# One more token tile, one less row buffer, and vector sums and routing moved between stages of a gated encoder block with product-key experts

## What is computed

```
h = x + (sig(gA) * Pool(xn) W_po + sig(gB) * Hyena(xn) W_ho) W_o,  xn = rmsnorm(x)
PEER:  q = rmsnorm(h) W_q;  s = q . keys   (8 heads, 2 halves, 128 keys each)
       top 16 of each half, then top 16 of the 256 sums -> 128 experts a token
       gate = softmax over each head's 16
       y = sum_e  gelu(u[idx_e] . xb) * gate_e * v[idx_e]
out = rmsnorm(h + y)
```

## Time and profile before

| | |
|---|---|
| median of 3 runs | 3104.2 us (3100.14 to 3113.33) |
| the profiled execution | 3101.03 us |
| its span, first to last instruction | 3098.9 us |
| granted TensorE clock, mean | 0.935 |
| TensorE / VectorE / ScalarE / GpSimd busy | 2656.7 / 2259.4 / 1064.1 / 1085.0 us |
| bytes moved by DMA | 998.59 MB, 322 GB/s over the span |
| fetches of rows | 640, 671.13 MB |

### The profile page before, as it was taken

One profiled execution on the slowest core, in us unless ns is written; L12 is line 12 of the kernel. 1 busy time (PEld: TensorE's weight loads), 2 busy tenths in 40 slices (PEclk: granted clock), 3 DMA queues, 4 the chain that ended last, 5 costly groups with the idle time before them and its releaser, 6 DMA issues.

```text
span 3098.9 us, 29223 instructions
## 1 busy us (share of the span) xinstructions
PE 2656.7 (86%) x9109; PEld 1651.5 (53%) x9109; DVE 2259.4 (73%) x4295; ACT 1064.1 (34%) x2757; POOL 1085.0 (35%) x694
## 2 busy tenths in 40 slices
PE   6999989698899988899567899889889988899884
PEld 4556647443344444455245566556566555566662
DVE  5341124776799894487987899878789997778778
ACT  4211122231234885774383222223222222223221
POOL 2211212132344332223333344434444444344443
PEclk9999999899899999999788999999999999999997
DMA  4332255397899999888899999999999999999997
GB/s 153 112 102 72 89 180 173 140 400 287 332 359 371 356 333 362 351 326 350 301 388 364 378 404 402 380 393 391 386 382 404 409 404 377 388 408 396 400 397 291
DMA packets 246385, 998.59 MB, mean 322 GB/s; under 512 B 20856, under 2 KB 99448, under 8 KB 161753
## 3 DMA queue, kind: packets, MB, share of 16 engines
q0 software_dynamic: 92160, 671.13, 54.3%
q1 hardware_dynamic: 152344, 300.45, 26.9%
q10 hardware_dynamic: 1728, 25.17, 2.0%
HBM read 950.26 MB, written 46.40 MB: 322 GB/s over the span
## 4 chain that ended last, share of the span: by engine, by line
PE 26%; DVE 22%; DMA 18%; issue 9%; ACT 4%; SPq 1%; POOL 0%; DVEq 0%; ACTq 0%
DMA arena<-in_peer_ut 13%; DVE h_tile L1803 8%; PE job_ps L1561 6%; DVE row L1792 5%; PE job_ps L687 4%; PE job_ps L1548 3%; DMA row<-in_peer_uv,row_u 2%; PE wide_ps L128 2%; PE wide_ps L129 2%; PE wide_ps L130 2%; PE wide_ps L687 2%; PE job_ps L1524 2%; DMA tmp_gates<-arena 1%; DVE uw_lo L1812 1%; ACT uw_hi L1663 1%
## 5 line engine op out<-in xcount | busy, mean ns | idle before, releaser
L1493 POOL DMA_INDIRECT row<-in_peer_uv,row_u x640 | 966.8, 1511 | 1506.2 <-DVE h_tile L1803 1101.5
L1792 DVE CUSTOM_DVE_ANT_0 row<-row,x_tile 128x1024 f32<-128x1024 f32 x640 | 778.3, 1219 | 124.2 <-DMA row<-in_peer_uv,row_u 106.3
L1561 PE MATMUL job_ps<-arena 128*128 128x512 f32 x1536 | 682.9, 594 | 10.6 <-DVE arena L1823 10.6
L1803 DVE SCALAR_TENSOR_TENSOR h_tile<-row,act_e,h_tile 128x1024 f32<-128x1024 f32 x512 | 654.4, 1278 | 13.4 <-ACT act_e L1680 12.8
L1676 ACT ACTIVATE gelu_e<-dots 128x1 f32<-128x1 f32 x640 | 128.2, 200 | 1230.5 <-DVE dots L1792 1230.0
L128 PE MATMUL wide_ps<-x_hi,uw_lo 128*128 128x384 f32 x1024 | 391.2, 382 | 156.0 <-DVE uw_lo L1812 155.3
L1561 PEld LDWEIGHTS job_ps<-arena 128*128 128x128 f32 x1536 | 290.2, 190 | 319.9 <-issue 308.6
L130 PE MATMUL wide_ps<-x_hi,uw_hi 128*128 128x384 f32 x1024 | 357.1, 349 | 0.0
L129 PE MATMUL wide_ps<-x_lo,uw_hi 128*128 128x384 f32 x1024 | 356.6, 348 | 0.0
L128 PEld LDWEIGHTS wide_ps<-x_hi,uw_lo 128*128 128x128 f32 x1024 | 203.4, 199 | 222.4 <-DVE uw_lo L1812 208.1
L1548 PE MATMUL job_ps<-row,diag 128*128 128x512 f32 x512 | 260.6, 640 | 54.9 <-ACT diag L1687 54.9
(11 more groups left out here) (252 smaller groups left out, 3026.8 us busy)
## 6 DMA issues: line engine op xcount, KB each, us to landing
arena<-in_peer_ut SPq DMA_DIRECT2D x128, 512.0 KB
arena<-in_peer_v SPq DMA_DIRECT2D x128, 512.0 KB
hand<-tmp_gates SPq DMA_DIRECT2D x32, 768.0 KB
tmp_gates<-arena ACTq DMA_DIRECT2D x10, 2048.0 KB
arena<-in_w_in SPq DMA_DIRECT2D x32, 512.0 KB, 3.5
hand<-in_w_in SPq DMA_DIRECT2D x32, 512.0 KB
row<-in_peer_uv,row_u POOLq DMA_INDIRECT x640
arena<-in_x SPq DMA_DIRECT2D x16, 512.0 KB, 5.8
```

The lines of the kernel that those rows point to most:

```text
L1493: pool.indirect_dma_start(row[n % NR][:], None, dram["peer_uv"], bass.IndirectOffsetOnAxis(row_u[g % 2][:, e:e + 1], 0)).then_inc(row_in[n ...
L1561: last = pe.matmul(job_ps[q][:], actd[j % 2][:, d * P:(d + 1) * P], vw[j % NO][:, half * 512:(half + 1) * 512], start=j == 0, stop=j == P - 1)
L1792: dve.tensor_tensor_reduce(out=mine, in0=mine, in1=xb[:], scale=1.0, scalar=0.0, op0=ALU.mult, op1=ALU.add, accum_out=dots[:, n % NA:n % N ...
L1803: dve.scalar_tensor_tensor(out=side, in0=row[n % NR][:, D:2 * D], scalar=act_e[:, n % NA:n % NA + 1], in1=side, op0=ALU.mult, op1=ALU.add) ...
```

## The change

Seven edits, made together:

1. `NR` goes from 7 row buffers to 6.
2. The token tile `x_tile` gets two buffers with a semaphore each. `load_x(g)` is issued 40 steps before the tile is needed instead of 1, and waits for the dots of the group before the last one instead of the last dot.
3. `by_pe` changes by quarters of 64 fetches: 1 of 4, 2 of 4, 2 of 4, 3 of 4 rows go to TensorE, instead of every second. There are still 128 of them: 48 of the first tile and 80 of the second. `sum_row` finds its first and last row of a tile from the counts.
4. A unit of kinds z, a, x, ga, gb and q of the second sequence is issued on TensorE in two parts of four products, so that other work of the loop can stand between them.
5. Routing of dense tile 3 starts at step 134 instead of 106; its exponentials move from 143 to 171, its gates from 147 to 175.
6. The 16 chunks of tile 3 move with them, from steps 159 to 204 to steps 178 to 223. The chunks of the other tiles stay, and so does everything after step 256.
7. The final sum of TensorE's part (`gathered`) asks for `g < 2` instead of the last row's kind.

```diff
--- before.py
+++ after.py
@@ -607,6 +607,8 @@
                 self.weight_ready(pe, wi)
                 self.free(pe, kind, n)
                 for k in range(KD):
+                    if self.ready and k == KD // 2:
+                        yield (self.begin[kind, n] + self.end[kind, n]) / 2
                     last = self.multiply(pe, self.bank(kind, n)[:], wi, k, (self.xn_hi, self.xn_lo), k, k == 0, k == KD - 1)
                 last.then_inc(self.w_used, 1)
             elif kind == "zt":
@@ -1230,10 +1232,10 @@
 
 def second_and_experts(nc, dram, R, small, handed, out):
 
-    NR, NSC, NW, NO = 7, 2, 3, 4
+    NR, NSC, NW, NO = 6, 2, 3, 4
     GJ, K, NA = 4, 3, 16
     ROWS = NG * P
-    by_pe = lambda n: n < 2 * P and n % 2 == 1
+    by_pe = lambda n: n < 2 * P and n % 4 in ((1,), (1, 3), (1, 3), (1, 2, 3))[n // (P // 2)]
     on_pe = lambda n: sum(by_pe(k) for k in range(n + 1))
     on_dve = lambda n: n + 1 - on_pe(n)
     CHUNKS = TD // 8
@@ -1248,17 +1250,17 @@
     now = lambda n: probe * n / LAST
     TURNED = next(n for n in range(ROWS) if now(n) >= sum(Pre.span([u], ()) for u in units if u[0] not in ("q", "s")))
     EARLY = CHUNKS // ND * 2
-    ROUTED = ((2, 68, 2), (3, 106, 2), (6, LAST + 50, 1), (7, 420, 1))
+    ROUTED = ((2, 68, 2), (3, 134, 2), (6, LAST + 50, 1), (7, 420, 1))
     CHOSEN = {1: (40, 1), 4: (LAST + 1, 4), 5: (LAST + 8, 2)}
-    RANKED_AT = (-1, 51, 105, 143, LAST + 4, LAST + 13, LAST + 124, 494)
-    GATED_AT = (0, 58, 108, 147, LAST + 6, LAST + 20, LAST + 130, 502)
+    RANKED_AT = (-1, 51, 105, 171, LAST + 4, LAST + 13, LAST + 124, 494)
+    GATED_AT = (0, 58, 108, 175, LAST + 6, LAST + 20, LAST + 130, 502)
     assert 191 < LAST and LAST + 20 < 2 * P - NR and LAST + 130 < 3 * P - NR and RANKED_AT[-1] < 4 * P - NR
-    X_AT = [P * g - 1 if g else 0 for g in range(NG)]
+    X_AT = [P * g - 40 if g else 0 for g in range(NG)]
     ADD_AT = [P * (g + 1) + K for g in range(NG)]
     NORM_AT = [max(ADD_AT[g] + 4, LAST + 5) for g in range(NG)]
     assert TURNED + 4 < X_AT[2] and all(NORM_AT[g] + 12 < P * (g + 2) for g in range(NG - 2))
     CHUNK_AT = [GATED_AT[2] + 3 + 3 * c for c in range(EARLY // 2)]
-    CHUNK_AT += [CHUNK_AT[-1] + 3 + 3 * c for c in range(EARLY // 2)]
+    CHUNK_AT += [max(CHUNK_AT[-1], GATED_AT[3]) + 3 + 3 * c for c in range(EARLY // 2)]
     CHUNK_AT += [max(CHUNK_AT[-1] + 3, GATED_AT[4]) + 3 + c + c // 2 for c in range(EARLY // 2)]
     BY_ACT = [c for c in range(CHUNKS) if c < EARLY or c % 2 == 0]
     BY_DVE = [c for c in range(CHUNKS) if c not in BY_ACT]
@@ -1284,7 +1286,7 @@
         m = Mem(nc, ctx)
         ctx.callback(m.release)
         row = [m.sb(f"row{b}", [P, 2 * D]) for b in range(NR)]
-        xb = m.sb("x_tile", [P, D])
+        xb = [m.sb(f"x_tile{b}", [P, D]) for b in range(2)]
         prod = [m.sb(f"prod{b}", [P, D]) for b in range(2)]
         rooms = [Room(prod[n]) for n in range(2)]
         ident = small.ident
@@ -1344,7 +1346,7 @@
         p.kf = [at(72 + 4 * b, 2, C) for b in range(2)]
         row_in = [m.sem(f"e_row_in{b}") for b in range(NR)]
         sc_in = [m.sem(f"e_sc_in{b}") for b in range(NSC)]
-        x_in, h_in = m.sem("e_x_in"), [m.sem(f"e_h_in{b}") for b in range(2)]
+        x_in, h_in = [m.sem(f"e_x_in{b}") for b in range(2)], [m.sem(f"e_h_in{b}") for b in range(2)]
         uw_in = [m.sem(f"e_uw_in{b}") for b in range(NW)]
         vw_in = [m.sem(f"e_vw_in{b}") for b in range(NO)]
         gt_in = [m.sem(f"e_gt_in{b}") for b in range(2)]
@@ -1386,9 +1388,9 @@
         def _(sp):
             def load_x(g):
                 tt = GATHERED[g]
-                if g:
-                    sp.wait_ge(dot_done, g * P)
-                sp.dma_start(xb[:], dram["xn2"][:, tt * D:(tt + 1) * D]).then_inc(x_in, 16)
+                if g >= 2:
+                    sp.wait_ge(dot_done, (g - 1) * P)
+                sp.dma_start(xb[g % 2][:], dram["xn2"][:, tt * D:(tt + 1) * D]).then_inc(x_in[g % 2], 16)
 
             def load_scores(r, hd):
                 k = r * H + hd
@@ -1542,11 +1544,12 @@
                 g, i = n // P, on_pe(n) - 1
                 pe.wait_ge(diag_done, i + 1)
                 pe.wait_ge(row_in[n % NR], 16 * (n // NR + 1))
-                if i % (P // 2) == 0 and g:
+                first, stop = i == on_pe(g * P - 1), on_pe(n) == on_pe((g + 1) * P - 1)
+                if first and g:
                     pe.wait_ge(summed_added, 2 * g)
                 for half in range(2):
                     last = pe.matmul(sum_ps[half][:], diag[i % 2][:], row[n % NR][:, D + half * 512:D + (half + 1) * 512],
-                                     start=i % (P // 2) == 0, stop=i % (P // 2) == P // 2 - 1)
+                                     start=first, stop=stop)
                 last.then_inc(row_summed, 1)
 
             def job(j):
@@ -1786,10 +1789,10 @@
             def dot(n):
                 g, e = n // P, n % P
                 if e == 0:
-                    dve.wait_ge(x_in, 16 * (g + 1))
+                    dve.wait_ge(x_in[g % 2], 16 * (g // 2 + 1))
                 dve.wait_ge(row_in[n % NR], 16 * (n // NR + 1))
                 mine = row[n % NR][:, 0:D]
-                dve.tensor_tensor_reduce(out=mine, in0=mine, in1=xb[:], scale=1.0, scalar=0.0,
+                dve.tensor_tensor_reduce(out=mine, in0=mine, in1=xb[g % 2][:], scale=1.0, scalar=0.0,
                                          op0=ALU.mult, op1=ALU.add, accum_out=dots[:, n % NA:n % NA + 1]).then_inc(dot_done, 1)
 
             def add_row(n):
@@ -1830,7 +1833,7 @@
 
             def gathered(g):
                 dve.wait_ge(row_added, on_dve((g + 1) * P - 1))
-                if by_pe((g + 1) * P - 1):
+                if g < 2:
                     dve.wait_ge(row_summed, on_pe((g + 1) * P - 1))
                     for q in range(2):
                         part = h[g % 2][:, q * 512:(q + 1) * 512]
```

## The result

| | before | the change |
|---|---|---|
| median, 7 runs each | 3113.3 us (3100.1 to 3117.6) | 3090.2 us (3083.6 to 3099.1) |
| ratio, 95% interval | | 0.9945 (0.9925 to 0.9964) |
| the profiled execution, its span | 3101.0 us, 3098.9 | 3098.6 us, 3096.5 |
| granted TensorE clock | 0.935 | 0.945 |

The ratio says 0.55% faster, 17 us (11 to 23), where I had forecast 25. The median of 3090.2 us lies 2 us above the forecast's own range (3050 to 3088) and inside the range with the rivals. The two profiles hide the gain: the one of before is among the fastest executions of its kernel, the one of the change is among the slowest of its own. So two totals of single profiles say little here. Stages do, when one kernel's stage differs from another's by more than the same stage differs between two executions.

A forecast was written before the change was run, and what follows sets the result against it. TensorE was taken to bound steps 0 to 224, VectorE 225 to 261, DMA the rest; the terms sum to -25 us, 3104.2 to 3079 us, range 3050 to 3088, with rivals 3042 to 3138.

The forecast's parts named there:

- 1 rows, steps 0 to 63: Steps 0 to 63: 16 rows on TensorE instead of 32 relieve TensorE, -18 us (0 to -33).
- 2 routing leaves 106 to 133: Steps 106 to 133: tile 3's routing leaves a window with TensorE and VectorE both full, -5 us (0 to -11).
- 3 fewer chunks, 128 to 191: Steps 128 to 191: 15 gate chunks instead of 21 free TensorE time, -20 us (-5 to -35).
- 4 fullest quarter, 192 to 224: Steps 192 to 224: 11 chunks instead of 5 and 24 rows instead of 16 load TensorE, +25 us (+20 to +45).
- 5 VectorE, 225 to 261: Steps 225 to 261: a quarter of the rows on VectorE instead of half, -8 us (0 to -10).
- 6 token tile early: Steps 128, 384, 512: early token tile removes dot waits and SP's queue gap, -15 us (-5 to -24).
- 7 units in parts: TensorE units: a row's sum stands behind half a unit, so VectorE starves less, -4 us (0 to -10).
- 8 six buffers, steps 0 to 261: Before the dense stage: fetches have three steps to land instead of four, +6 us (0 to +30).
- 8 six buffers, dense stage: From step 262: fetches have three steps to land instead of four, +14 us (0 to +60).
- the rival that I built on the lead: Steps 64 to 127 and dense stage: fetches outlast three steps, rows come late, 3132 us in all; chance 0.17.
- The first rival: Steps 0 to 191: half of the 43 us gain stays away through DMA and lockstep, 3100 us; chance 0.30.

The follow-up runs named there:

- b_rows: Kernel before with only the new pattern of rows on TensorE; ratio 0.9979 to before.
- a_oldrows: The change without its new pattern of rows on TensorE (every second row up to 255 again); ratio 0.9971 to before.
- a_oldroute: The change with routing, gates and chunks of tile 3 at their old steps; ratio 0.9936 to before.
- six_only: Kernel before with one edit, six row buffers instead of seven; ratio 0.9999 to before.
- b_throttle6: Kernel before, seven buffers, but from fetch 262 on a fetch waits until row n-6 is used; ratio 0.9923 to before.
- s7_thr6: The change with seven buffers, one late-loaded token tile, and from fetch 262 on a wait for row n-6; ratio 0.9881 to before.
- six_x2: Kernel before with six row buffers and two token tiles loaded 40 steps early; ratio 1.0006 to before.
- s7_rest: The change with seven row buffers and one token tile, loaded late; ratio 0.9937 to before.
- control_before: Kernel before once more, unchanged, for a second profile; steps 0 to 261 took 1059.7 us there.
- s7_thr5: The change with seven buffers, one late-loaded token tile, and from fetch 262 on a wait for row n-5; ratio 1.048 to before.

## Why the prediction was off, by its own steps

The direction was right; the size was 25 us where 17 came. Step by step (the profiles' numbers scatter as said above):

| step of the sum | forecast | measured, and by what |
|---|---|---|
| 1 rows, steps 0 to 63 | -18 | -9 (`b_rows`, `a_oldrows`) |
| 2 routing leaves 106 to 133 | -5 | -1 in the change, steps 64 to 133 (`a_oldroute`) |
| 3 fewer chunks, 128 to 191 | -20 | -13, steps 134 to 191 (`a_oldroute`) |
| 4 fullest quarter, 192 to 224 | +25 | +12 by chunks, +2 by rows |
| 5 VectorE, 225 to 261 | -8 | -1 to -4 |
| 6 token tile early | -15 | -8 in the profiles, not seen in the ratios |
| 7 units in parts | -4 | -10 by the ratios (4 to 18) |
| 8 six buffers, steps 0 to 261 | +6 | +24 to +33 in the profiles, in the change +24 to +37 |
| 8 six buffers, dense stage | +14 | -13 to -25 (`six_only`, `b_throttle6`, `s7_thr6`) |

In two groups, by the ratios: steps 1 to 5 and 7, the work that moves, were to give 30 us and gave 19 to 20. Steps 6 and 8, buffers and token tiles, were to cost 5 us and cost 2 (`six_x2`, -4 to +8). So the total is short because of the first group. That the second came close is luck: its two buffer terms were off by some 20 and some 30 us, in opposite directions, and the errors cancel.

**Steps 1 to 3 failed by their limit, and this is the step that made the forecast too large.** They took TensorE as what sets the length of steps 0 to 191: 43 us were to go there and 23 went. In steps 0 to 63 TensorE's busy time fell by 19 us (209.3 to 190.1), and the stage did not follow. What freed the rows changed hands. Fetches waited 83.7 us for TensorE and 69.5 for VectorE in the kernel before (608 to 853 us); with the new pattern alone (`b_rows`) they wait 35.0 for TensorE and 104.9 for VectorE, which now does the additions:

```profile
POOL row L1493 <- DVE h_tile L1804: 104.9, 46, 9.0
POOL row L1493 <- PE job_ps L1549: 35.0, 4, 23.9
```

I had checked only that VectorE has time for these additions (187 of 242 us), not when they free a row. How much of the 9 us that are missing there comes from this was not measured by itself. With seven buffers half of step 1 came true, and steps 2 and 3 nearly as forecast: `s7_rest` and `s7_thr6` take 240 us in steps 64 to 133 (kernels with six buffers 245 and more, the one before 251.7) and 84 to 85 in steps 159 to 177, where the change takes 90.1 and the kernel before 100.0. In the change six buffers took a part of it back.

**Step 4** was too large by half: TensorE took the moved work with almost no gap left (136.3 of 139.6 us), as the lower bound had it, but its busy time rose by 19.6 us where my unit prices gave 31.3. The granted clock of the stage rose from 0.94 to 1.00, which may be a part of it; what is missing stays open.

**Step 8 failed in kind in the dense stage.** I wrote that a fetch that isn't in the queue "leaves its bandwidth to the U loads", and used this only to make a loss small. I bounded the cost by 0 from below. In a stage where the earlier trace rows showed twelve times as much waiting for tables as for rows, the early rows were the excess, and a gain should have been inside the bounds. And the rival that I built on the lead (three steps against a fetch time of about 11 us) was priced with a late fetch, 13.0 us. The median of all 640 fetches is 9.7 us on the page of `control_before` and 9.5 with three steps to land, under the 11 us from which the rival decides.

**Step 8 was mis-sized before step 262**: +6 where the profiles show +24 to +33, and even the lowest reading by the ratios is +14. I looked at the average length of a step (3.6 to 3.8 us and more) and not at its spread. In steps 0 to 261 some rows are freed by TensorE, behind a unit or behind the one block of unit "i", which is 27 us long, and the buffers bridge just these gaps. In the change (up to 1640 us) fetches still wait 303.4 us for TensorE and 359.9 for VectorE (344.3 and 312.6 before), and dots wait 137.7 us for rows instead of 92.5:

```profile
DVE row L1795 <- DMA row<-in_peer_uv,row_u: 137.7, 76, 16.0
```

**The first rival** (it cancels) said that half of the gains in steps 0 to 191 would not come. That is what happened: 23 of 43 us came, and the missing 20 are what the rival had taken off. Whether by its cause, DMA and the lockstep with VectorE, is not shown. The change still came out better than the rival's 3100 us, because step 4 cost 11 us less than forecast and step 7 gave more. The gain in the dense stage, which no part of the sum had but for the token tile, went to pay for six buffers before it.

## What to carry to other kernels

When a stage is bound by DMA and two streams share it, compare how long the consumer waits for each: the stream that is hardly ever late may be fetched too early, and a bound on how far it may run ahead can be worth more than its buffer. Such a bound is one wait and can be set by stage; a buffer less is set for the whole kernel and costs wherever the rows are freed unevenly. Look also at which loads of the late stream are late, and what stands ahead of them in their queue. Before adding up an edit's gains over an engine's busy time, ask what frees the buffers that the others wait for. And when an edit makes something scarcer, the lower end of its price is not zero but what the thing takes from others.

## What the runs showed of the hardware

The mean rate of DMA over a stage depends on how many fetches may be under way, and not in one direction. Between 1700 and 3000 us it was 393 GB/s with up to five fetches of 1 MB under way (`control_before`), 401 with up to four (`b_throttle6`), 352 with up to three (`s7_thr5`). Of these three the middle one is best for this mix. The holes behind late table loads are part of the reason: in the first ten microseconds of the one shown above DMA moved 414 GB/s and in the next five 190, while the change's window around step 512, which has no hole, had 416. The median time of a 1 MB fetch changes little, 9.7 us with four steps to land, 9.5 with three and 8.4 with two. The slowest U load changes more, 33.3 us with four steps and 25.6 with three.
